# Delta mixer: filler in a bank without readers, gate mixed in the receptance loop, rate evacuated in one run, VectorE's products between value tiles

## The chip, the cores and the metric

The kernel runs on one core of one Trainium2 chip. The metric is the device time of one execution in microseconds (us). Three runs of the kernel before gave a median of 2432.17 us (2429.4 to 2437.03).

## The reference, cut to what matters

The program computes two blocks of a small network on 256 tokens of width 1024. The first block (feed-forward layers and two kinds of attention) and most of the second are not touched. The change lies in the one layer of the second block that mixes tokens with the generalised delta rule:

```
xx = x_prev - x                       # x_prev: x shifted by one token
r = (x + xx*mu[0]) @ w_rkv[0]         # receptance
k = (x + xx*mu[2]) @ w_rkv[1]         # key
v = (x + xx*mu[3]) @ w_rkv[2]         # value
xw, xa, xg = x + xx*mu[1], x + xx*mu[4], x + xx*mu[5]
w_log = -softplus(-(w0 + tanh(xw @ w1) @ w2)) - 0.5;  decay = exp(-exp(w_log))
a = sigmoid(a0 + (xa @ a1) @ a2)      # rate
g = sigmoid(xg @ g1) @ g2             # gate
kk = normalised per head(k * k_k);  k = k * (1 + (a - 1) * k_a)
# per head and token: state = state*w + (state @ -kk) outer (kk*a) + v outer k;  y = state @ r
out = group_norm(y) + (sum over the head of r*k*r_k) * v
return (out * g) @ w_o
```

The recurrence is computed in chunks of 64 tokens, from products of r, k, kk and a with exponentials of the summed decay.

## The kernel before, in words

Activations lie with the width on the partitions: a tensor of 1024 x 256 is eight tiles of 128 x 256 (`KD` = 8). A weight chunk is 128 x 1024 and holds what one output tile needs. SyncE loads chunks into a ring of eight (line 463, `weight_ring`). For float32 accuracy each chunk of the three large projections is cut into an upper part, which ScalarE writes (line 2119, `weight_upper`, four slots), and a rest, which VectorE writes (line 1395, `weight_lower`). An output tile is 24 matmuls of 128x256: lower x upper, upper x lower, upper x upper for eight tiles of input. All matmuls are issued from the helper at line 517, whatever calls it; transposes stand at line 1196.

There is no planner that runs on the chip: every engine works through an order written out by hand. One thing is placed by a rule, though. Before a wait, ScalarE and VectorE call `due`, which first cuts weight chunks up to three cuts past the chunk that TensorE had taken at the event waited for. So the place of an instruction `dve.wait_ge(*due(event))` in VectorE's text also sets where VectorE cuts the next chunks: it cuts them there and not earlier.

TensorE writes to eight PSUM banks. The helper `refill(b)` makes it wait until the readers of bank b's last content are done; `next_bank` goes round banks 0 to 3. `hold(b, n)` issues n matmuls of the identity into bank b, which nobody reads; they only keep the engine at work. Each starts with `refill(b)`.

The mixer's stages, in TensorE's order: `lora_in(3)` (decay, eight input tiles `xs_t[3]`, two fillers ahead of each), `lora_in(4)` (rate), `lora_up(3)`, the eight key tiles (project_all of items(1), the first three of them interleaved), `lora_up(4)`, `lora_in(5)` (gate), the head sums of kk, `lora_up(5)`, the eight receptance tiles with the spread of the kk norms after the fifth, the eight value tiles with the head sums of the bonus after the seventh, then `delta_core`, which begins with transposes of v (line 1196) and the spread of the bonus.

Ahead of the mixer the helper `spread_two` spreads two norms into banks 6 and 7; VectorE reads bank 7 at line 1769 when it writes the normed input `xn` (name `xn_t` in the trace), tile by tile, and the bank's reader is the event after the last tile.

VectorE's order: the mixed inputs of decay and rate (line 1889, `shifted(3, k)`, `shifted(4, k)`); for key and receptance `shifted` at line 1893 and the rest of the split at line 1428 (`shifted_halves`); then the eight tiles of the gate's input (line 1889, `shifted(5, k)`), which read what ScalarE's `part(5, k)` (line 2430) wrote; then `shifted_halves(2)` for the value; the norms of kk (lines 1919 to 1932); the scans of the decay (line 1925); and, once ScalarE has written `exp_plus` (line 2479), eight products `rkr` (line 1939), `bt` (line 1942), `ar[:, 1]` (line 1943), the copy of 32 columns `w_end` (line 1944), and after the head sums of the bonus two steps (lines 1947 and 1880) and `ar[:, 0]` (line 1950).

ScalarE, for the key: per tile two evacuations (lines 2457, 2458), the receptance's upper part `xs_upper(0, f)` (line 2134), `part(5, f)` (line 2430). Then per tile the evacuation of the rate (line 2322, `lora_raw (4, k)`) and `xs_upper(2, k)`. For the value tiles: the exponentials at lines 2478, 2479 and 2482 and the evacuations (line 2322). GpSimd does `kk` (line 2626), `before_sum` (line 2630), `k_mixed` (line 2634), `kk_a` (line 2639) and, after `bt`, `k_scaled` (line 2642) as one instruction of 128x2048.

Of the kernel before, what the change touches and what calls it, by code (L numbers as in the profile page):

```python
# [7 lines left out]
ALU = mybir.AluOpType  # L8
ACT = mybir.ActivationFunctionType
# [31 lines left out]
CH = 64  # L41
# [155 lines left out]
def program(nc, dram, out, seen, stream):  # L197

    ctx = ExitStack()
    with ctx:  # L200
# [272 lines left out]
        def _(pe):  # L473
# [660 lines left out]
            def delta_mixer(i):  # L1134
# [3 lines left out]
                def lora_in(j, wd):  # L1138
                    w, used = arrived("lora1", j - 3, KD * wd)
                    b = next_bank()  # L1140
                    for k in range(KD):
                        if j == 3:
                            hold(7, 2)
                        pe.wait_ge(*of("xs", (j, k)))
                        mn = mm(bank[0:wd, b, 0:S], w[:, k * wd:(k + 1) * wd], xs_t[j][:, k, :],
                                k == 0, k == KD - 1)
# [40 lines left out]
            def delta_core():  # L1187
# [3 lines left out]
                for m, src in enumerate((v_t, ar[:, 0], bt, kt_)):  # L1191
# [8 lines left out]
                    if m == 0:  # L1200
                        head_spread("bonus", at=4)
                        pe.wait_ge(*of("ar", 0))
                        pe.wait_ge(*of("k_scaled", 0))

# [175 lines left out]
        def _(dve):  # L1380
# [514 lines left out]

            def shifted_halves(j):

                for k in range(KD):
                    shifted(j, k)
                    for done in [k - 1] * (k > 0) + [k] * (k == KD - 1):  # L1900
                        lower(xs_hl[j], done, xs_t[j][:, done, :], ("xs_upper", (j, done)), ("xs_lower", (j, done)))

            def delta_mixer(i):
# [7 lines left out]
                dve.wait_ge(*due("rkv_raw", (4, KD - 1)))  # L1911
                shifted_halves(0)
                for k in range(KD):
                    shifted(5, k)
                dve.wait_ge(*due("rkv_raw", (1, KD - 1)))
# [20 lines left out]
                for k in range(KD):  # L1936
                    dve.wait_ge(*due("rkv", (0, k)))
                    dve.wait_ge(*due("k_mixed", k))
                    V.scalar_tensor_tensor(rkr_t[:, k, :], r_t[:, k, :], vec("r_k", k), k_t[:, k, :],
                                           ALU.mult, ALU.mult).then_inc(*did("rkr", k))  # L1940
                dve.wait_ge(*due("kk_a", 3))
                step(V.tensor_tensor(bt, aa_t, kt_, ALU.mult), [("b_scaled", 0)])
                step(V.tensor_tensor(ar[:, 1], r_t, exp_plus, ALU.mult))
                step(V.tensor_copy(w_end[:, :, :],
                                   exp_plus.rearrange("p k (c t) -> p k c t", t=CH)[:, :, :, CH - 1]))
                dve.wait_ge(*due("head_sums", "bonus"))
                step(V.tensor_copy(stat[:, 1, :], bank[:, 6, 0:QT * RH]), [("head_sums_read", "bonus")])
                widen("bonus", 1)
                dve.wait_ge(*due("exp_before", 0))
                V.scalar_tensor_tensor(ar[:, 0], kk_t, -1.0, sg_t, ALU.mult, ALU.mult).then_inc(*did("ar", 0))  # L1950
                for b in range(4):
# [152 lines left out]
        def _(act):  # L2104
# [319 lines left out]
            def delta_mixer(i):  # L2424
# [29 lines left out]
                for f in range(KD):  # L2454
# [3 lines left out]
                    A.activation(k_t[:, f, :], ps, ACT.Copy).then_inc(*did("rkv", (1, f)))  # L2458
                    xs_upper(0, f)
                    act.wait_ge(*due("xs_lower", (1, f)))  # L2460
                    part(5, f)
                for k in range(KD):
                    evac("lora_raw", (4, k), aa_t[:, k, :], "lora_out", ACT.Sigmoid, bias=vec("a0", k))
                    xs_upper(2, k)
                lora(5, P, ACT.Sigmoid)
# [9 lines left out]
                for f in range(KD):  # L2475
# [4 lines left out]
                    elif f == 2:  # L2480
                        act.wait_ge(*due("before_sum", KD - 1))
                        A.activation(sg_t, sg_t, ACT.Exp, scale=-E_HALF).then_inc(*did("exp_before", 0))
                    evac("rkv_raw", (2, f), v_t[:, f, :], "rkv")
# [80 lines left out]
        def _(pool):  # L2564
# [53 lines left out]
            for i in range(DEPTH):  # L2618
                if i == 1:
# [21 lines left out]
                    pool.wait_ge(*of("b_scaled", 0))  # L2641
                    G.tensor_tensor(kt_, kt_, k_t, ALU.mult).then_inc(*did("k_scaled", 0))
                    for n in range(4):
# [125 lines left out]
```

## Time and profile before

| | us |
|---|---|
| median of three runs | 2432.17 |
| the profiled execution | 2437.4 |
| its span | 2435.5 |
| TensorE busy in the span | 2310.4 (95%) |
| VectorE, ScalarE, GpSimd busy | 1584.6, 1173.9, 362.4 |

The chain of work that ended last is TensorE for 80% of the span, VectorE for 9%, ScalarE for 5%. The mean granted TensorE clock is 0.97 of full speed. The mixer lies between 1790 and 2100 us of the span; the change touches 1793 to 1940. In the rows below, a start is in us from the span's start, a row with xN merges N instructions that follow one another, and the bracket at the end is the idle time of that engine before it and what ended it.

### The profile page before, as it was taken

The numbers are of one execution on the slowest core, as the hardware profiler recorded it, in microseconds if no ns is written. First come the engines' busy times: TensorE is split into PE (matmuls) and PEld (weight loads), VectorE is DVE, ScalarE is ACT, GpSimd is POOL, SyncE is SP. The second block draws the span as 40 slices with busy tenths as digits, with TensorE's granted clock in tenths as the row PEclk, the third lists the DMA queues.
The fourth block names the chain that finished last, engine by engine and source line by source line (L and its number), as shares of the span: only waits on it lengthen the run. The fifth ranks groups of instructions, "written<-read, shape, count | busy, mean of one in ns | idle before, by whom it ended". The sixth has DMA issues, their size and how long they took to land.

```text
span 2435.5 us, 41847 instructions
## 1 busy us (share of the span) xinstructions
PE 2310.4 (95%) x17252; PEld 2041.5 (84%) x17252; DVE 1584.6 (65%) x2226; ACT 1173.9 (48%) x2043; POOL 362.4 (15%) x353
## 2 busy tenths in 40 slices
PE   7999998899999999988999999999989798999998
PEld 7888977788888889777888999688868788978887
DVE  5886766578778866665776686277556553545763
ACT  3654443455546544444655575365446321445542
POOL 0110012111101100210111102020222230022001
PEclk9999998899999999989999999999998899999999
DMA  7776742257758767423566544355524300333553
GB/s 268 286 261 234 257 169 96 82 187 262 241 200 289 253 225 266 169 82 102 173 224 216 174 160 161 107 170 184 180 86 131 104 3 3 123 129 119 193 181 104
DMA packets 114237, 417.19 MB, mean 171 GB/s; under 512 B 12672, under 2 KB 12928, under 8 KB 113664
## 3 DMA queue, kind: packets, MB, share of 16 engines
q1 hardware_dynamic: 113184, 409.56, 49.4%
q10 hardware_dynamic: 864, 4.96, 0.6%
q8 instruction: 138, 2.26, 0.4%
q14 instruction: 51, 0.42, 0.1%
HBM read 413.42 MB, written 1.05 MB: 170 GB/s over the span
## 4 chain that ended last, share of the span: by engine, by line
PE 80%; DVE 9%; ACT 5%; issue 4%; POOL 2%; DMA 1%; POOLq 0%; DVEq 0%; ACTq 0%
PE banks L517 79%; DVE weight_lower L1395 2%; ACT weight_upper L2119 1%; ACT heap L2238 1%; DVE weight_ring L1406 1%; POOL heap L2584 1%; PE banks L908 0%; DVE nmax L1552 0%; DVE heap L1550 0%; DVE heap L1533 0%; ACT L2153 0%; DMA consts<-consts_dram 0%; DVE xn_t L1623 0%; DMA weight_ring<-ffn_up_dram 0%; DVE silu L1617 0%
## 5 line engine op out<-in xcount | busy, mean ns | idle before, releaser
L517 PE MATMUL banks<-xn_halves,weight_upper 128*128 128x512 f32 (+1 forms) x3680 | 1016.3, 347 | 8.5 <-DVE weight_lower L1395 6.5
L1395 DVE TENSOR_TENSOR weight_lower<-weight_ring,weight_upper 128x1024 fp32r<-128x1024 f32 x580 | 736.3, 1276 | 330.0 <-ACT weight_upper L2119 328.7
L517 PE MATMUL banks<-xn_halves,weight_lower 128*128 128x256 f32 x2832 | 807.4, 285 | 23.6 <-DVE branch_a_lower L1587 13.0
L2119 ACT ACTIVATE weight_upper<-weight_ring 128x1024 fp32r<-128x1024 f32 x580 | 609.5, 1056 | 344.3 <-PE banks L517 226.1
L517 PEld LDWEIGHTS banks<-xn_halves,weight_upper 128*128 128x128 f32 x3680 | 648.5, 193 | 97.5 <-DVE weight_lower L1395 6.8
L517 PEld LDWEIGHTS banks<-xn_halves,weight_lower 128*128 128x128 f32 x2832 | 544.5, 192 | 32.6 <-DVE branch_a_lower L1587 15.1
L517 PE MATMUL banks<-hidden,weight_upper 128*128 128x512 f32 x1216 | 429.2, 398 | 4.9 <-DVE heap L1474 4.2
L517 PE MATMUL banks<-hidden,weight_lower 128*128 128x256 f32 x1216 | 341.4, 281 | 0.0
L517 PEld LDWEIGHTS banks<-hidden,weight_upper 128*128 128x128 f32 x1216 | 228.3, 188 | 61.8 <-DVE heap L1474 5.2
L2584 POOL TENSOR_TENSOR heap<-heap 128x256 f32<-128x256 f32 x120 | 121.4, 1016 | 960.8 <-ACT heap L2335 634.0
L517 PEld LDWEIGHTS banks<-hidden,weight_lower 128*128 128x128 f32 x1216 | 229.7, 189 | 0.0
L1406 DVE CUSTOM_DVE_ANT_0 weight_ring<-weight_ring,c_rows,vecs 128x1024 f32<-128x1024 f32 x144 | 187.3, 1302 | 32.5 <-DMA weight_ring<-w_ada_dram 30.1
L517 PE MATMUL banks<-heap 64*64 64x64 f32 (+10 forms) x2432 | 184.4, 265 | 16.9 <-ACT heap L2244 4.8
L517 PEld LDWEIGHTS banks<-heap 64*64 64x64 f32 (+5 forms) x2432 | 154.0, 151 | 44.1 <-issue 29.1
L2573 POOL TENSOR_TENSOR heap<-heap 128x256 f32<-128x256 f32 x88 | 68.0, 772 | 511.3 <-ACT heap L2182 510.7
L517 PE MATMUL banks<-heap,weight_ring 64*64 64x15 f32 (+3 forms) x944 | 119.6, 295 | 0.0
L517 PE MATMUL banks<-consts 128*128 128x128 f32 x816 | 110.4, 290 | 5.4 <-DVE xn_t L1769 5.4
L517 PEld LDWEIGHTS banks<-heap,weight_ring 64*64 64x64 f32 (+3 forms) x944 | 96.3, 162 | 22.1 <-issue 5.9
L517 PEld LDWEIGHTS banks<-consts 128*128 128x128 f32 x816 | 102.7, 203 | 9.4 <-issue 8.9
L2177 ACT ACTIVATE heap<-banks 128x512 f32<-128x512 f32 x88 | 52.5, 597 | 116.6 <-PE banks L517 116.6
L1474 DVE TENSOR_TENSOR heap<-banks,heap 128x512 f32<-128x512 f32 x88 | 60.8, 691 | 47.6 <-ACT heap L2177 47.6
L2238 ACT ACTIVATE heap<-heap,nmax 128x256 f32<-128x256 f32 (+2 forms) x128 | 52.0, 408 | 60.9 <-DVE nmax L1555 60.8
(287 smaller groups left out, 2605.7 us busy)
## 6 DMA issues: line engine op xcount, KB each, us to landing
weight_ring<-w_ada_dram SPq DMA_DIRECT2D x144, 512.0 KB, 4.4
weight_ring<-ffn_gate_dram SPq DMA_DIRECT2D x88, 512.0 KB, 3.6
weight_ring<-ffn_up_dram SPq DMA_DIRECT2D x88, 512.0 KB, 3.6
weight_ring<-ffn_down_dram SPq DMA_DIRECT2D x88, 512.0 KB, 3.5
weight_ring<-m_w_up_dram SPq DMA_DIRECT2D x64, 512.0 KB, 3.7
weight_ring<-m_w_down_dram SPq DMA_DIRECT2D x64, 512.0 KB, 3.7
weight_ring<-w_in_dram SPq DMA_DIRECT2D x58, 512.0 KB, 4.3
weight_ring<-b_w_rkv_dram SPq DMA_DIRECT2D x24, 512.0 KB, 3.6
```

The source lines that it names most:

```text
L517: return nc.tensor.matmul(o, w, r, start=first, stop=last)
L1395: V.tensor_tensor(w_lo[:, n % RING, :], ring[:, n % RING, :], w_hi[:, j % SPLITS, :].bitcast(F32), ALU.subtract).then_inc(*did("weight_low ...
L1406: V.tensor_tensor_reduce(w, w, c_rows[:, :], half, vec("b_ada", i), ALU.mult, ALU.add, mod[:, i:i + 1]).then_inc(*did("ada_mod", i, also=[ ...
L1474: V.tensor_tensor(gu[:, f % 4], bank[:, b:b + 2, 0:S], gu[:, f % 4], ALU.add).then_inc(*did("gate_up", (s, f)))
L2119: A.activation(w_hi[:, j % SPLITS, :], ring[:, n % RING, :], ACT.Copy).then_inc(*did("weight_upper", j))
L2177: A.activation(gu[:, f % 4], bank[:, b:b + 2, S:2 * S], ACT.Copy).then_inc(*did("gate_up_half", (s, f)))
L2238: A.activation(s_, s_, ACT.Exp, bias=nmax[:, u % 2, j:j + 1], accum_out=den[:, u % 2, j:j + 1]).then_inc(*did("exp", (l, u, j), also=[("ex ...
L2573: G.tensor_tensor(gu[:, f % 4, 0, :], gu[:, f % 4, 0, :], gu[:, f % 4, 1, :], ALU.mult).then_inc(*did("hidden", (s, f)))
L2584: G.tensor_tensor(acc, acc, sum_tile(n, what, f), ALU.add).then_inc(*did("sum_added", (n, what, f)))
```

## The change

- Filler: the two fillers ahead of each input tile of `lora_in(3)` go to bank 5, not bank 7.
- Gate: `shifted(5, k)` moves from a loop of its own into the loop of `shifted_halves(0)`, right behind `shifted(0, k)`. On ScalarE `part(5, f)` now stands ahead of `xs_upper(0, f)`.
- Rate: ScalarE evacuates the eight tiles `lora_raw (4, k)` in one run, and writes the eight `xs_upper(2, k)` behind them.
- Products: VectorE gets waits on the evacuated value tile 0 ahead of `bt`, tile 2 ahead of `ar[:, 1]`, tile 3 ahead of `ar[:, 0]`, which moves ahead of the bonus steps. The copy `w_end` moves to ScalarE, behind the exponential of line 2482. GpSimd's `k_scaled` becomes eight instructions of 128x256; TensorE waits for the last.

```diff
 lora_in, TensorE
-                            hold(7, 2)
+                            hold(5, 2)
 delta_core, TensorE
-                        pe.wait_ge(*of("k_scaled", 0))
+                        pe.wait_ge(*of("k_scaled", KD - 1))
 VectorE
-            def shifted_halves(j):
+            def shifted_halves(j, other=None):
                 for k in range(KD):
                     shifted(j, k)
+                    if other:
+                        shifted(other, k)
                     for done in [k - 1] * (k > 0) + [k] * (k == KD - 1):
                         lower(xs_hl[j], done, ...)
...
-                shifted_halves(0)
-                for k in range(KD):
-                    shifted(5, k)
+                shifted_halves(0, 5)
...
+                dve.wait_ge(*due("rkv", (2, 0)))
                 dve.wait_ge(*due("kk_a", 3))
                 step(V.tensor_tensor(bt, aa_t, kt_, ALU.mult), [("b_scaled", 0)])
+                dve.wait_ge(*due("rkv", (2, 2)))
                 step(V.tensor_tensor(ar[:, 1], r_t, exp_plus, ALU.mult))
-                step(V.tensor_copy(w_end[:, :, :], exp_plus...[:, :, :, CH - 1]))
+                dve.wait_ge(*due("rkv", (2, 3)))
+                dve.wait_ge(*due("exp_before", 0))
+                V.scalar_tensor_tensor(ar[:, 0], kk_t, -1.0, sg_t, ALU.mult, ALU.mult).then_inc(*did("ar", 0))
                 dve.wait_ge(*due("head_sums", "bonus"))
                 step(V.tensor_copy(stat[:, 1, :], bank[:, 6, 0:QT * RH]), [("head_sums_read", "bonus")])
                 widen("bonus", 1)
-                dve.wait_ge(*due("exp_before", 0))
-                V.scalar_tensor_tensor(ar[:, 0], kk_t, -1.0, sg_t, ALU.mult, ALU.mult).then_inc(*did("ar", 0))
 ScalarE
-                    xs_upper(0, f)
                     act.wait_ge(*due("xs_lower", (1, f)))
                     part(5, f)
+                    xs_upper(0, f)
                 for k in range(KD):
                     evac("lora_raw", (4, k), aa_t[:, k, :], "lora_out", ACT.Sigmoid, bias=vec("a0", k))
+                for k in range(KD):
                     xs_upper(2, k)
...
-                        A.activation(sg_t, sg_t, ACT.Exp, scale=-E_HALF).then_inc(*did("exp_before", 0))
+                        A.activation(sg_t, sg_t, ACT.Exp, scale=-E_HALF)
+                        act.wait_ge(*due("exp_plus", 0))
+                        A.activation(w_end[:, :, :], exp_plus...[:, :, :, CH - 1],
+                                     ACT.Copy).then_inc(*did("exp_before", 0))
 GpSimd
-                    G.tensor_tensor(kt_, kt_, k_t, ALU.mult).then_inc(*did("k_scaled", 0))
+                    for k in range(KD):
+                        G.tensor_tensor(kt_[:, k, :], kt_[:, k, :], k_t[:, k, :], ALU.mult).then_inc(
+                            *did("k_scaled", k))
```

## Rows read from the trace of the kernel before

**Rows 1.** The waits view, TensorE alone, 1785 to 1965 us: total, times, longest.
```profile
PE banks L517 <- DVE weight_lower L1395: 11.5, 1, 11.5
PE banks L517 <- DVE xn_t L1769: 5.4, 1, 5.4
```
**Rows 2.** The timeline, TensorE, lora_in(3) and lora_in(4).
```profile
1798.39 1.19 PE L517 MATMUL banks<-consts 128*128 128x128 f32 x4 [5.37 <-DVE xn_t L1769]
...
1802.68 0.71 PE L517 MATMUL banks<-consts 128*128 128x128 f32 x4
...
1809.40 4.10 PE L517 MATMUL banks<-heap,weight_ring 128*64 128x256 f32 x18
```
**Rows 3.** The timeline, VectorE: inputs (line 1889) of xs_t[3], then of xs_t[4].
```profile
1793.40 0.48 DVE L1889 SCALAR_TENSOR_TENSOR heap<-xn_t,vecs,heap 128x255 f32<-128x255 f32 x1
...
1794.58 0.85 DVE L1889 SCALAR_TENSOR_TENSOR heap<-xn_t,vecs,heap 128x255 f32<-128x255 f32 x1
...
1797.78 0.47 DVE L1769 SCALAR_TENSOR_TENSOR xn_t<-x_t,vecs,banks 128x256 f32<-128x256 f32 x1
...
1800.56 4.03 DVE L1889 SCALAR_TENSOR_TENSOR heap<-xn_t,vecs,heap 128x255 f32<-128x255 f32 x8
```
**Rows 4.** Stretches of 2 us: engines' busy (xcount), granted clock, DMA share, GB/s.
```profile
1796.00:1798.00 2.00, 0.00 (x0) 0.00 (x0) 2.00 (x6) 1.37 (x3) 2.00 (x4) 0.50 0.00 0
1846.00:1848.00 2.00, 1.33 (x5) 0.59 (x4) 2.00 (x3) 1.46 (x5) 1.01 (x1) 1.00 0.65 238
1908.00:1910.00 2.00, 0.00 (x0) 0.00 (x0) 2.00 (x2) 2.00 (x4) 0.00 (x0) 1.00 0.71 258
```
**Rows 5.** The timeline, TensorE: the end of lora_up(4), lora_in(5), lora_up(5).
```profile
1852.18 2.92 PE L517 MATMUL banks<-silu,weight_ring 64*128 64x256 f32 x6 [3.98 <-ACT heap L2322]
1855.04 6.43 PE L517 MATMUL banks<-heap,weight_ring 128*128 128x256 f32 x16
...
1865.55 6.28 PE L517 MATMUL banks<-silu,weight_ring 128*128 128x256 f32 x16
```
**Rows 6.** The timeline, VectorE: part of a round of the key loop, then the gate's inputs.
```profile
1842.37 0.83 DVE L1428 TENSOR_TENSOR shifted_lower<-heap,shifted_upper 128x256 fp32r<-128x256 f32 x1
...
1843.52 1.21 DVE L1395 TENSOR_TENSOR weight_lower<-weight_ring,weight_upper 128x1024 fp32r<-128x1024 f32 x1
...
1847.69 3.23 DVE L1889 SCALAR_TENSOR_TENSOR heap<-xn_t,vecs,heap 128x255 f32<-128x255 f32 x8
```
**Rows 7.** The timeline, ScalarE: the last key round's start, then the rate's tiles.
```profile
1844.65 1.11 ACT L2119 ACTIVATE weight_upper<-weight_ring 128x1024 fp32r<-128x1024 f32 x1
...
1846.92 0.53 ACT L2322 ACTIVATE heap<-banks,vecs 128x256 f32<-128x256 f32 x1
1851.35 0.42 ACT L2134 ACTIVATE shifted_upper<-heap 128x256 fp32r<-128x256 f32 x1 [3.89 <-DVE heap L1893]
1851.68 0.46 ACT L2322 ACTIVATE heap<-banks,vecs 128x256 f32<-128x256 f32 x1
```
**Rows 8.** The timeline, ScalarE, VectorE and GpSimd around TensorE's pause in the value tiles.
```profile
1904.28 1.04 ACT L2119 ACTIVATE weight_upper<-weight_ring 128x1024 fp32r<-128x1024 f32 x1
...
1904.41 3.90 DVE L1939 SCALAR_TENSOR_TENSOR xn_t<-heap,vecs 128x256 f32<-128x256 f32 x8 [5.28 <-ACT heap L2479]
...
1910.60 6.60 POOL L2642 TENSOR_TENSOR heap<-heap 128x2048 f32<-128x2048 f32 x1 [5.34 <-DVE heap L1942]
...
1912.88 4.36 DVE L1944 COPY w_end<-heap 128x32 f32<-128x32 f32 x1
1917.27 4.63 DVE L1395 TENSOR_TENSOR weight_lower<-weight_ring,weight_upper 128x1024 fp32r<-128x1024 f32 x4
```
**Rows 9.** The timeline, TensorE: the bonus sums and the first transposes.
```profile
1931.68 3.63 PE L517 MATMUL banks<-consts,xn_t 128*128 128x2 f32 x32
...
1940.56 1.94 PE L1196 MATMUL banks<-consts,heap 128*128 128x128 f32 x16 [0.78 <-ACT heap L2322]
```
**Rows 10.** The timeline, VectorE: a cut in the receptance loop, beside GpSimd's work.
```profile
1876.60 1.68 DVE L1395 TENSOR_TENSOR weight_lower<-weight_ring,weight_upper 128x1024 fp32r<-128x1024 f32 x1 [2.14 <-ACT weight_upper L2119]
```

More of the change, by code:

```diff
@@ L1940, in delta_mixer @@
                                            ALU.mult, ALU.mult).then_inc(*did("rkr", k))
+                dve.wait_ge(*due("rkv", (2, 0)))
                 dve.wait_ge(*due("kk_a", 3))
                 step(V.tensor_tensor(bt, aa_t, kt_, ALU.mult), [("b_scaled", 0)])
+                dve.wait_ge(*due("rkv", (2, 2)))
                 step(V.tensor_tensor(ar[:, 1], r_t, exp_plus, ALU.mult))
-                step(V.tensor_copy(w_end[:, :, :],
-                                   exp_plus.rearrange("p k (c t) -> p k c t", t=CH)[:, :, :, CH - 1]))
+                dve.wait_ge(*due("rkv", (2, 3)))
+                dve.wait_ge(*due("exp_before", 0))
+                V.scalar_tensor_tensor(ar[:, 0], kk_t, -1.0, sg_t, ALU.mult, ALU.mult).then_inc(*did("ar", 0))
                 dve.wait_ge(*due("head_sums", "bonus"))
@@ L2481, in delta_mixer @@
                         act.wait_ge(*due("before_sum", KD - 1))
-                        A.activation(sg_t, sg_t, ACT.Exp, scale=-E_HALF).then_inc(*did("exp_before", 0))
+                        A.activation(sg_t, sg_t, ACT.Exp, scale=-E_HALF)
+                        act.wait_ge(*due("exp_plus", 0))
+                        A.activation(w_end[:, :, :], exp_plus.rearrange("p k (c t) -> p k c t", t=CH)[:, :, :, CH - 1],
+                                     ACT.Copy).then_inc(*did("exp_before", 0))
                     evac("rkv_raw", (2, f), v_t[:, f, :], "rkv")
```

## The prediction

> **What bounds the kernel now.** The page comes first: TensorE is busy 95% of the span and carries 80% of the chain that ended last, so a change to the mixer pays only where TensorE stands still or works at a low clock. The waits view of TensorE names two pauses, 11.5 us for a cut weight chunk and 5.4 us for line 1769 [rows 1]; the timeline adds a third, 3.98 us for an evacuation of ScalarE [rows 5], and places all three.
>
> Pause A lies ahead of `lora_in(3)`: TensorE idles from 1793.0 to 1798.39 [rows 2]. Its releaser is the last normed tile, written by 1798.25, although the first input xs_t[3] is there at 1793.88 [rows 3]. TensorE doesn't wait for data; it waits to overwrite bank 7 with filler. Pause B lies in `lora_up(4)` and ends at 1852.18 [rows 5]. Followed back: the bank wants the rate's second evacuation (1851.68), which stands behind an `xs_upper(2, 0)` that waited 3.89 us for VectorE [rows 7], which ran the eight gate tiles from 1847.69 to 1850.9 first [rows 6]. Pause C, 11.5 us from 1907.1 on, lies behind the third value tile: VectorE doesn't come to cutting the fourth value chunk before 1917.27, and TensorE starts when the first of four cuts is done, at 1918.55 [rows 1, 8].
>
> Pauses also cost clock. Late in A the granted clock is at the lower level (1.2 GHz) [rows 4]; a round of fillers and one input tile then takes 2.15 us (two from 1798.39 to 1802.68), and 1.21 at the upper level (2.4 GHz), as in the five and a half up to 1809.40 [rows 2]. Behind B a matmul of 128x256 takes 0.40 (16 in 6.43) where 0.23 (18 in 4.10) is the upper level's [rows 2, 5].
>
> **The change, part by part.** Times are on the axis of the execution before; a gain in one stage moves the later ones as a block.
>
> *Filler in bank 5.* Bank 5 held nothing but filler just before, so the wait goes, and what is late next is the input. TensorE starts at 1793.0; tile 0 is there at 1793.88 and tile 1 at 1795.43, so rounds 0 and 1 end near 1794.6 and 1796.1. From there on inputs come every 0.8 us, the last near 1800.1 [rows 3], faster than a round of 1.21: six rounds end at 1803.4. `lora_in(4)` is 16 matmuls of 0.225, 3.6 us, and ends at 1807.0; its inputs are all there by 1804.6 [rows 3]. Before, it ended at 1813.5 [rows 2]. **Gain 6.5**, and not more, since work and inputs fill the stretch. The other end: should the clock fall in the thin first rounds for as long as it was low before, two rounds cost 0.9 more each: 4.6.
>
> *Gate in the receptance loop, rate in one run.* The eight gate tiles cost VectorE 3.2 us wherever they stand; what counts is what waits behind them. In the key loop VectorE's lines 1428 and 1893 take 1.15 from start to start (1842.37 to 1843.52) and the cut 1.13, a round of 2.28 [rows 6]; ScalarE's round is 2.27 (1844.65 to 1846.92) [rows 7]. Both catch up behind TensorE's 2.88 (24 matmuls of 0.12), since the first three key tiles come at once. With a gate tile (0.40) VectorE's round is 2.68, still under 2.88, so key tiles aren't starved. But `xs_upper(0, f)` waits for VectorE, so ScalarE falls to its pace in the last five rounds: at most 2.0 us later, and I take 1.4, because `part(5, f)` now fills some of that wait. The first rate evacuation comes at 1848.3, not 1846.92 [rows 7]. Nothing stands between the eight any more, at 0.36 each, so `lora_up(4)` gets its last bank near 1849.9 and `lora_in(5)` starts at 1850.5, not 1855.04: 4.5 saved. What the clock adds is open. If it stays up, `lora_in(5)` takes 3.6 and not 6.4, but another thing ends last then: the value's upper parts now follow the evacuations, VectorE makes their inputs from about 1850.9 in eight rounds of 0.73, to 1856.8, and the gate's Sigmoid stands behind them on ScalarE, at 1857. So `lora_up(5)` starts no earlier than 1857.0 to 1857.8, where it was 1865.55 [rows 5], and the head sums ahead of it may pull the clock down, as the bonus sums do: the value tile behind them takes 4.6, not 2.9 (1935.2 to 1939.8) [rows 9]. That caps the gain at 8.6. Ends 4.5 (clock as before) and 8.6; I take the middle, since TensorE would be half busy and never long idle from 1846 to 1850.5, and a stretch like that kept its clock (1846 to 1848 [rows 4]). **Gain 6.5.** The moved uppers cost nothing for the value tiles, which come 40 us later; without that cover they would cost what they take, eight of 0.35.
>
> *Products between value tiles.* Before, VectorE is done with `rkr` at 1908.3; `bt` takes 2.29, up to GpSimd's release at 1910.60, `ar[:, 1]` as long, and the copy of 32 columns 4.36 [rows 8]. The copy ends at 1917.24 and GpSimd's `k_scaled` at 1917.20: the copy stood waiting for GpSimd. Now the wait on value tile 0 (evacuated right behind the upper cut of 1904.28, so no wait in fact) makes VectorE cut the fourth chunk at 1908.3, and the tile starts at 1909.6: a pause of 2.5 us for 11.5. Then come `bt` (to 1911.8), two cuts, `ar[:, 1]`, a cut, `ar[:, 0]`, a cut, with eight instructions of GpSimd beside them. A cut takes 1.21 alone [rows 6] and 1.68 beside GpSimd [rows 10]; I charge each VectorE instruction behind `bt` with a whole piece of GpSimd, 0.7 (an eighth of some 5 us, what is left of 6.60 when `ar[:, 1]`'s share is off it). The cuts end at 1913.8, 1915.7 and, behind `ar[:, 1]` (1918.7), at 1920.6. Value tiles 3 to 6 run 1909.6 to 1912.5, 1913.8 to 1916.7, to 1919.6, and 1920.6 to 1923.5. The bonus sums take 3.5 and the last tile 4.6 [rows 9]: 1931.6, for 1939.8. **Gain 8.2.** Without the charge for GpSimd the count gives 1929.9, a gain of 9.9; with the clock down after the short pause (the four tiles from 1918.55 took 13.1 to 1931.68, not 11.5) it gives 6.6. `w_end` costs ScalarE less than an evacuation of 256 columns, 0.36, and is hidden by TensorE's next tile; uncovered it would cost that. `ar[:, 0]` ends earlier than before, and the last piece of `k_scaled` is wanted only behind the first transposes.
>
> The Trainium skill, SBUF — State Buffer, section SBUF: two separate sides, says that VectorE and GpSimd share one port pair as an exclusive lock, for a VectorE instruction with two SBUF inputs too, and the loser stands still for the other's whole instruction. It speaks against `k_scaled` in eight: each piece is one more turn that a cut can lose. By it the value stage gives between the 8.2 and the 9.9 just worked out. The trace agrees: the copy ends with GpSimd's instruction.
>
> Sum: 6.5 + 6.5 + 8.2 = 21.2 us; ends 4.6 + 4.5 + 6.6 = 15.7 and 6.5 + 8.6 + 9.9 = 25.0. The profiled execution took 2437.4 (1.9 around its span); its like would take 2416.2. It stands 5.2 above the median of 2432.2, which becomes 2411.0.
>
> **The rivals.**
> - *The key loop tips over.* If both the cut (1.68) and line 1428 wait for GpSimd, VectorE's round is 1.68 + 1.15 + 0.40 = 3.2. Five rounds of 3.2, not 2.28, put the first rate evacuation at 1851.5: pause B is moved, not removed, and that stage gives 0.7. In all 15.4: 2416.8. For it: neither engine has slack there [rows 6, 7]. Against: the present round holds one such wait already.
> - *Clock not kept.* Fed in pieces, TensorE stays at the lower level: eight rounds of 2.15 and 7.2 for `lora_in(4)` end at 1817.4, 4.0 later than now; the others give their low ends. 7.1 in all: 2425. Against: the same pattern ran at the upper level from 1802.7 on [rows 2], and 1 to 3 us into pause C the clock was still up [rows 4].
> - *The filler's wait stays*, because bank 5 has a reader after all: 14.7 in all, 2417.5. The text of the kernel speaks against it.
> - *Slower.* The lower clock spreads over every stage that is fed in pieces: 4.0 lost at `lora_in`; key tiles 4 to 8 at 0.213 a matmul, 5.1 a tile, 11.2 lost; the value stage gives nothing (1909.6 + 4 x 5.1 + 4.4 + 5.1 = 1939.5); 4.5 of the rate stage is left. 10.7 slower: 2443. It decides where VectorE's key round passes 2.88 and each tile starts with a pause. Against: TensorE would still be busy 90% there.
>
> **How the numbers follow.** Forecast 0.72; key loop 0.12; clock not kept 0.06; filler 0.03; slower 0.04; more than 25 us, by a clock that is up throughout, 0.03. The predicted time is the forecast's, 2411. Its ends are 2407.2 and 2416.5; key loop and filler lie at 2416.8 and 2417.5; with 3 us for the scatter of medians the range is 2404 to 2420, which leaves out the clock rivals. About 0.3% (7.3 us) can be told from no change: faster 0.72 + 0.12 + 0.03 + 0.03 = 0.90, within it 0.06, slower 0.04.
>
> **What would show it.** Right: no wait for line 1769 in TensorE's waits view; waits for `weight_lower` in the value tiles of 2 to 5 us in all, the longest near 2.5; ScalarE's eight rate evacuations 0.36 apart; `k_scaled` as eight pieces with cuts of 1.7 or more beside them. Wrong: a granted clock of 0.5 from `lora_in(5)` through `lora_up(5)` (then that stage gives 4.5), a late cut in the key loop, or the time won handed back at a wait in `delta_core`, which I don't see.

## The result, and the profile after

The changed kernel is faster, by less than forecast. Over six runs each, measured side by side, its median is 2419.1 us (2410.7 to 2425.5) and that of the kernel before 2434.2: a ratio of 0.9935, interval 0.991 to 0.996, or 15 us. Forecast were 2411 and 21 us. The profiled execution took 2425.5 us with a span of 2423.5; forecast for its like were 2416.2.

TensorE's waits over the same stretch (who waited for whom: total, times, longest):

```profile
PE banks L517 <- DVE weight_lower L1395: 2.7, 2, 2.4
PE banks L517 <- ACT heap L2459: 1.2, 1, 1.2
PE banks L517 <- ACT heap L2323: 1.2, 2, 0.9
PE banks L517 <- DVE heap L1889: 0.7, 2, 0.5
```

Against [rows 1], the wait for line 1769 is gone, that for cut chunks fell from 11.5 to 2.7, and pause B (3.98 in [rows 5]) became two of 1.2 and 0.9. The lines of ScalarE and GpSimd moved by one to six: 2119 is now 2120, 2322 is 2323, 2642 is 2648.

TensorE's timeline of the changed kernel, from the last fillers to `lora_up(3)`, and then the rate and gate stage:

```profile
1792.50 3.29 PE L517 MATMUL banks<-consts 128*128 128x128 f32 x28
1796.25 0.65 PE L517 MATMUL banks<-heap,weight_ring 128*64 128x256 f32 x2 [0.46 <-DVE heap L1889]
...
1809.13 1.99 PE L517 MATMUL banks<-silu,weight_ring 64*128 64x256 f32 x8
...
1840.98 1.56 PE L517 MATMUL banks<-silu,weight_ring 64*128 64x256 f32 x6
1843.78 0.91 PE L517 MATMUL banks<-silu,weight_ring 64*128 64x256 f32 x2 [1.24 <-ACT heap L2459]
1845.60 3.78 PE L517 MATMUL banks<-silu,weight_ring 64*128 64x256 f32 x8 [0.91 <-ACT heap L2323]
1849.31 6.20 PE L517 MATMUL banks<-heap,weight_ring 128*128 128x256 f32 x16
1855.35 4.60 PE L517 MATMUL banks<-consts,heap 128*128 128x2 f32 x32
1859.81 6.07 PE L517 MATMUL banks<-silu,weight_ring 128*128 128x256 f32 x16
```

Stage A is clean: the fillers run straight on, and the wait for the first input is 0.46 us. The rate stage is not: `lora_in(5)` and `lora_up(5)` take about as long as in [rows 5].

The value tiles: the timeline of ScalarE, VectorE, GpSimd and TensorE, to set beside [rows 8, 9].

```profile
1902.25 1.21 DVE L1395 TENSOR_TENSOR weight_lower<-weight_ring,weight_upper 128x1024 fp32r<-128x1024 f32 x1
1902.53 0.26 ACT L2486 ACTIVATE w_end<-heap 128x32 f32<-128x32 f32 x1
1903.38 2.27 DVE L1943 TENSOR_TENSOR heap<-heap 128x2048 f32<-128x2048 f32 x1
1905.69 2.90 DVE L1395 TENSOR_TENSOR weight_lower<-weight_ring,weight_upper 128x1024 fp32r<-128x1024 f32 x2
1905.74 13.64 POOL L2648 TENSOR_TENSOR heap<-heap 128x256 f32<-128x256 f32 x8 [6.47 <-DVE heap L1943]
1908.52 2.82 DVE L1945 TENSOR_TENSOR heap<-heap 128x2048 f32<-128x2048 f32 x1
...
1903.51 0.38 PE L517 MATMUL banks<-shifted_upper,weight_lower 128*128 128x256 f32 x1 [2.41 <-DVE weight_lower L1395]
1906.97 0.38 PE L517 MATMUL banks<-shifted_upper,weight_lower 128*128 128x256 f32 x1 [0.33 <-DVE weight_lower L1395]
1916.05 3.94 PE L517 MATMUL banks<-consts,xn_t 128*128 128x2 f32 x32
1926.10 1.94 PE L1196 MATMUL banks<-consts,heap 128*128 128x128 f32 x16 [0.78 <-ACT heap L2323]
```

VectorE cuts right behind `rkr`, the long pause is 2.41 us, and the copy costs ScalarE 0.26.

To compare kernels I cut the stretch at starts of TensorE's instructions in each timeline; "whole" runs from the first normed tile (line 1769) to the first transposes. Microseconds:

| kernel | first normed tile to lora_up(3) | to first key tile | to lora_up(4) | to lora_in(5) | to receptance | to bonus sums | to transposes | whole |
|---|---|---|---|---|---|---|---|---|
| before | 22.4 | 6.7 | 24.5 | 10.5 | 16.5 | 60.2 | 8.9 | 149.5 |
| after | 15.8 | 6.7 | 25.1 | 8.3 | 16.2 | 50.5 | 10.1 | 132.7 |
| filler_only | 15.8 | 6.7 | 25.0 | 10.5 | 13.4 | 60.3 | 8.9 | 140.4 |
| gate_rate_only | 23.0 | 6.7 | 24.8 | 8.3 | 16.0 | 60.0 | 8.9 | 147.8 |
| products_only | 23.0 | 6.7 | 24.8 | 10.4 | 13.3 | 50.5 | 8.9 | 137.6 |
| after_again | 15.8 | 6.7 | 25.9 | 8.3 | 13.4 | 50.5 | 8.9 | 129.5 |
| rate_fillers | 15.8 | 6.7 | 25.2 | 6.7 | 12.1 | 51.1 | 7.4 | 124.9 |
| one_k_scaled | 15.8 | 6.7 | 25.7 | 8.3 | 13.2 | 54.3 | 10.1 | 134.2 |
| copy_on_vector | 15.8 | 6.7 | 25.7 | 8.3 | 13.3 | 51.2 | 10.4 | 131.3 |
| no_waits | 15.8 | 6.7 | 24.6 | 7.1 | 16.5 | 56.4 | 8.9 | 136.0 |
| gate_apart | 15.8 | 6.7 | 25.2 | 6.4 | 12.2 | 51.1 | 7.4 | 124.7 |
| late_sums | 15.8 | 6.7 | 25.7 | 8.3 | 13.3 | 55.0 | 4.4 | 129.2 |
| key_fillers | 15.8 | 7.2 | 23.2 | 6.7 | 13.7 | 50.5 | 10.1 | 127.2 |
| gate_apart_fillers | 15.8 | 7.2 | 23.2 | 5.8 | 12.1 | 51.1 | 7.4 | 122.5 |

In late_sums the bonus sums stand behind the eighth value tile, so its last two columns count differently. Within a column the entries of kernels with the same edit there mostly agree to 0.1 us. The columns that don't (to lora_up(4), to receptance, to transposes) are those where the clock changes, and they differ between two traces of one and the same kernel (after, after_again) by up to 3 us. Single entries of the others move with the clock too. In no_waits, the 7.1 ahead of `lora_in(5)` stands beside 8.3 in six traces with the same code there: the pauses are as long, but the clock fell only 1.3 us behind the second of them, and the last eight matmuls of `lora_up(4)` took 2.56 us and not 3.78. The first column has 22.4 and 23.0 without the filler's edit.

### The profile page after: what moved, and what is told of

Same layout as the page of the kernel before. It is cut to its first block, busy times and chain, and to the rows that moved or that the text cites. A ratio compares the mean times of both kernels' runs of the same rounds, so it can differ in the third digit from the quotient of the medians.

```text
span 2423.5 us, 41857 instructions
## 1 busy us (share of the span) xinstructions
PE 2314.7 (96%) x17252; PEld 2042.7 (84%) x17252; DVE 1581.6 (65%) x2225; ACT 1173.8 (48%) x2044; POOL 369.3 (15%) x360
## 4 chain that ended last, share of the span: by engine, by line
PE 81%; DVE 8%; ACT 4%; issue 4%; POOL 2%; DMA 1%; POOLq 0%; DVEq 0%; ACTq 0%
PE banks L517 80%; DVE weight_lower L1395 2%; ACT heap L2239 1%; DVE weight_ring L1406 1%; POOL heap L2589 1%; ACT weight_upper L2120 1%; PE banks L908 0%; DVE nmax L1552 0%; DVE heap L1550 0%; DVE heap L1533 0%; ACT L2154 0%; DMA weight_ring<-ffn_up_dram 0%; DMA c_rows<-c_rows_dram 0%; PE banks L1196 0%; ACT heap L2284 0%
## 5 line engine op out<-in xcount | busy, mean ns | idle before, releaser
L517 PEld LDWEIGHTS banks<-xn_halves,weight_lower 128*128 128x128 f32 x2832 | 545.5, 193 | 32.3 <-DVE branch_a_lower L1587 15.1
```

The lines of the kernel that those rows point to most:

```text
L517: return nc.tensor.matmul(o, w, r, start=first, stop=last)
```

## The experiments

**Each part alone, and the changed kernel once more on the same chip.** The edits are the hunks of the diff.

`filler_only`:

```diff
-                            hold(7, 2)
+                            hold(5, 2)
```

> The kernel before with one edit: the fillers of lora_in(3) go to bank 5. From the first normed tile to the start of lora_up(3) the kernel before takes 22.4 us. My theory (TensorE waited to overwrite bank 7, not for data): 15.8, and the 6.6 us stay won up to the transposes (149.5 becomes 142.9, or up to 2 us off that by the clock); the run is 0.2 to 0.3% faster, 5 to 7 us. Rival (bank 7 was not what it waited for): 22.4 and no change.

Measured: 2430.7 us, ratio 0.9977 (0.9961 to 0.9993), and 15.8 us in the first column. The wait for line 1769 is gone from its waits view. The 6.6 us are there, in this kernel and in every one with the edit (15.8 in the table). The whole is 9.1 us shorter, more than the 2 us of margin that I gave: 3.1 of it lie between `lora_in(5)` and the receptance, where nothing was edited.

`gate_rate_only` has the gate tiles in the loop of `shifted_halves(0, 5)`, ScalarE's changed order, and the rate in one run.

```diff
-                shifted_halves(0)
-                for k in range(KD):
-                    shifted(5, k)
+                shifted_halves(0, 5)
```

> The kernel before with the edits on the gate and the rate alone. From the start of lora_up(4) to the start of lora_in(5) it takes 10.5 us before and 8.3 in the changed kernel; from there to the first receptance tile 16.5 and 16.2. My theory (the pause is shorter, but the clock falls all the same): 8.3 and 16.2 again, 2 us in all. Rival (this edit is worth 4.5 to 8.6 by itself, as forecast, and was spoiled by the phase that the filler's edit gave it): 4 to 8 us less over the two stretches.

Measured: 2437.7 us, ratio 1.000 (0.9976 to 1.0023); 8.3 and 16.0 in its two columns. The theory holds: this part is worth 2.1 us, by itself as in company, too little for the medians. The phase of the other edits didn't spoil it.

`products_only` has the waits, the order, the copy on ScalarE and the eight pieces.

```diff
+                dve.wait_ge(*due("rkv", (2, 0)))
...
+                dve.wait_ge(*due("rkv", (2, 2)))
...
-                    G.tensor_tensor(kt_, kt_, k_t, ALU.mult).then_inc(*did("k_scaled", 0))
+                    for k in range(KD):
+                        G.tensor_tensor(kt_[:, k, :], kt_[:, k, :], k_t[:, k, :], ALU.mult).then_inc(
+                            *did("k_scaled", k))
```

> The kernel before with the edits of the value tiles alone (waits, order, the copy on ScalarE, GpSimd in eight pieces). From the first receptance tile to the transposes the kernel before takes 69.1 us, the changed one 60.6. Theory: 60.6 here too, 8.5 us by itself, since the stage doesn't lean on the other edits; the run 0.3 to 0.35% faster. Rival (part of it came from the earlier stages): under 6 us.

Measured: 2427.6 us, ratio 0.9957 (0.9936 to 0.9978). From the receptance to the transposes 59.4 us, 9.7 less than before: the part doesn't lean on the others. In every kernel that keeps this part whole and the sums in their place, the bonus sums come 9.1 or 9.7 earlier; the rest is the clock of the last value tile (8.9, 10.1 or 7.4 in the last column).

`after_again` is the changed kernel, without an edit.

> The changed kernel, unchanged, on the same chip as the three parts. If the parts add up: 6.6 + 2 + 8.5 = 17 us from the first normed tile to the transposes, 149.5 becoming 132.7, and 15 us in the medians. If the parts overlap or spoil one another by the clock, the sum of the three alone differs from this by over 2 us.

Measured: 2421.8 us, ratio 0.9933 (0.991 to 0.9955), and 129.5 for the whole, 20.0 less than before, not 16.8. The three parts alone give 9.1 + 1.8 + 11.9 = 22.8, over 2 us off. Both gaps are one column: from `lora_in(5)` to the receptance. Without it the parts give 6.1 + 1.3 + 8.8 = 16.2 and the whole edit 16.5 and 16.9. So the parts add up, and the clock deals out 3 us on top. TensorE's timeline of after_again:

```profile
1851.44 3.78 PE L517 MATMUL banks<-silu,weight_ring 64*128 64x256 f32 x8 [1.12 <-ACT heap L2323]
1855.15 5.02 PE L517 MATMUL banks<-heap,weight_ring 128*128 128x256 f32 x16
1860.00 3.63 PE L517 MATMUL banks<-consts,heap 128*128 128x2 f32 x32
1863.49 5.39 PE L517 MATMUL banks<-silu,weight_ring 128*128 128x256 f32 x16
```

The last three took 6.20, 4.60 and 6.07 above, the same instructions behind nearly the same pauses (1.25 and 1.12 us here, 1.24 and 0.91 there).

**Keeping TensorE at work in lora_up(4).**

```diff
 lora_up
                     for f in range(KD):
+                        if j == 4 and f in (3, 4):
+                            hold(5, 5)
                         b = next_bank()
```

> The changed kernel with five fillers into bank 5 ahead of the fourth and of the fifth matmul of lora_up(4), where TensorE pauses 1.24 and 0.91 us. Theory (the clock, lost in these pauses, is the term that was mis-sized): the granted clock stays 1.0 through lora_in(5), which takes 3.6 us and not 6.0; the stretch from the start of lora_up(4) to the first receptance tile goes from 24.5 to 18 to 21, 4 to 6 us won. Rival (ScalarE's pace sets it: evacuations, then uppers of the value ahead of the gate's Sigmoid): lora_in(5) gets faster but lora_up(5) starts as late as before, under 1.5 us won.

Measured: 2413.4 us, ratio 0.9894 (0.984 to 0.9949), an interval that reaches the changed kernel's 0.9935; the time won is read from the traces. In TensorE's timeline of rate_fillers five fillers show as ten instructions:

```profile
1842.99 1.38 PE L517 MATMUL banks<-consts 128*128 128x128 f32 x10
1844.32 0.70 PE L517 MATMUL banks<-silu,weight_ring 64*128 64x256 f32 x2
1844.94 1.38 PE L517 MATMUL banks<-consts 128*128 128x128 f32 x10
1846.26 1.99 PE L517 MATMUL banks<-silu,weight_ring 64*128 64x256 f32 x8
1848.18 3.72 PE L517 MATMUL banks<-heap,weight_ring 128*128 128x256 f32 x16
```

Two stretches of 2 us of the same kernel, and then two of the changed one: the stretch and its length, busy times of TensorE, weight loads, VectorE, ScalarE and GpSimd, the granted clock, DMA share, GB/s. A clock of 1.00 is the upper level, 2.4 GHz, and 0.50 the lower, 1.2.

```profile
1846.00:1848.00 2.00, 2.00 (x11) 1.55 (x10) 2.00 (x6) 2.00 (x7) 0.00 (x0) 1.00 0.00 0
1848.00:1850.00 2.00, 2.00 (x10) 1.63 (x9) 1.17 (x4) 1.42 (x5) 0.00 (x0) 1.00 0.35 63
```
```profile
1846.00:1848.00 2.00, 2.00 (x6) 1.52 (x6) 1.73 (x5) 1.41 (x4) 0.00 (x0) 0.50 0.00 0
1850.00:1852.00 2.00, 2.00 (x6) 1.58 (x5) 1.77 (x5) 1.10 (x4) 0.00 (x0) 0.50 0.74 248
```

The same eight matmuls take 1.99 and not 3.78, and the sixteen of `lora_in(5)` 3.72 and not 6.20. From the start of `lora_up(4)` to the receptance it is 18.8 us, against 24.5 and 21.7 in the two traces of the changed kernel. The fillers add matmuls and win 2.9 to 5.7 us: the clock was the larger part of what the stage lost, and the rival (ScalarE's pace, under 1.5 us) falls. The clock then falls behind the head sums, so `lora_up(5)` still takes 5.2.

**The value stage taken apart.** Three kernels from the changed one.

```diff
-                        pe.wait_ge(*of("k_scaled", KD - 1))
+                        pe.wait_ge(*of("k_scaled", 0))
...
-                    for k in range(KD):
-                        G.tensor_tensor(kt_[:, k, :], kt_[:, k, :], k_t[:, k, :], ALU.mult).then_inc(
-                            *did("k_scaled", k))
+                    G.tensor_tensor(kt_, kt_, k_t, ALU.mult).then_inc(*did("k_scaled", 0))
```

> The changed kernel with k_scaled as one instruction of 128x2048 again. If GpSimd's instruction and VectorE's of two SBUF inputs exclude each other for whole instructions: k_scaled starts at bt's end and runs some 4.4 us, the cuts of value tiles 4 and 5 stand behind it, and TensorE gets a second pause of about 2.5 to 3 us ahead of value tile 4; the stretch from the receptance's start to the transposes is 2 to 3 us longer than the 60.6 of the changed kernel. If they share: no more than 0.5 us longer, and the cuts are only slower by a part.

Measured: 2426.8 us, ratio 0.9956 (0.9927 to 0.9986); from the receptance to the transposes 64.4, not 60.6: 3.8 longer. The timeline of VectorE, GpSimd and TensorE:

```profile
1899.83 6.75 DVE L1395 TENSOR_TENSOR weight_lower<-weight_ring,weight_upper 128x1024 fp32r<-128x1024 f32 x2
1899.87 5.62 POOL L2647 TENSOR_TENSOR heap<-heap 128x2048 f32<-128x2048 f32 x1 [6.47 <-DVE heap L1943]
...
1906.63 0.43 PE L517 MATMUL banks<-shifted_upper,weight_lower 128*128 128x256 f32 x1 [2.39 <-DVE weight_lower L1395]
```

Two cuts that take 2.4 alone took 6.75, so 4.4 went into standing behind GpSimd; its 5.62 are 1.2 of waiting for the first cut and those 4.4 of work. One stood still while the other worked. The pause of 2.39 us is the one expected; the stretch was to be 2 to 3 us longer and is 3.8, and what goes beyond the pause is clock, at 0.50 from 1908 to 1910. The Trainium skill, SBUF — State Buffer, section SBUF: two separate sides, states such an exclusive lock for the whole instruction; this trace agrees (6.75 = 2 x 1.2 + 4.4).

```diff
+                step(V.tensor_copy(w_end[:, :, :],
+                                   exp_plus.rearrange("p k (c t) -> p k c t", t=CH)[:, :, :, CH - 1]))
...
-                        A.activation(sg_t, sg_t, ACT.Exp, scale=-E_HALF)
-                        act.wait_ge(*due("exp_plus", 0))
-                        A.activation(w_end[:, :, :], exp_plus.rearrange("p k (c t) -> p k c t", t=CH)[:, :, :, CH - 1],
-                                     ACT.Copy).then_inc(*did("exp_before", 0))
+                        A.activation(sg_t, sg_t, ACT.Exp, scale=-E_HALF).then_inc(*did("exp_before", 0))
```

> The changed kernel with the copy of 32 columns back on VectorE, behind ar[:, 1]; waits and eight pieces kept. Theory (the 4.36 us were a wait for GpSimd's one long instruction): the copy now takes at most one piece of GpSimd, under 1.3 us, and the stretch from the receptance's start to the transposes stays within 1 us of 60.6. Rival (such a copy is slow by itself): 4 us and a pause of TensorE of 2 us or more.

Measured: 2417.0 us, ratio 0.9925 (0.9895 to 0.9956); 61.6 us in the stretch, 1.0 longer. VectorE's timeline:

```profile
1899.72 0.60 DVE L1946 COPY w_end<-heap 128x32 f32<-128x32 f32 x1
```

The same copy of 32 columns took 4.36 in [rows 8]. It was never slow; it waited for GpSimd. Once GpSimd works in pieces, moving the copy to ScalarE is worth 0.7 us up to the bonus sums (50.5 for 51.2); the last column differs by the clock.

`no_waits`:

```diff
-                dve.wait_ge(*due("rkv", (2, 0)))
                 dve.wait_ge(*due("kk_a", 3))
...
-                dve.wait_ge(*due("rkv", (2, 2)))
...
-                dve.wait_ge(*due("rkv", (2, 3)))
```

> The changed kernel without the three new waits on value tiles in VectorE's text, all else kept. If the waits do the placing of the cuts: VectorE cuts the fourth value chunk only behind bt, ar[:, 1] and ar[:, 0], near 7 to 9 us after rkr ends, and TensorE's pause is 8 to 10 us in place of 2.4; the stretch from the receptance's start to the transposes is 6 to 8 us longer than 60.6. If the moved copy was what mattered, it is at most 2 us longer.

Measured: 2424.3 us, ratio 0.9933 (0.9905 to 0.9961); 65.3 in the stretch, 4.7 longer, with one pause of 7.5 us. VectorE's timeline:

```profile
1910.41 2.29 DVE L1943 TENSOR_TENSOR heap<-heap 128x2048 f32<-128x2048 f32 x1
1912.73 3.29 DVE L1395 TENSOR_TENSOR weight_lower<-weight_ring,weight_upper 128x1024 fp32r<-128x1024 f32 x2
1915.95 2.81 DVE L1945 SCALAR_TENSOR_TENSOR heap<-spare,heap 128x2048 f32<-128x2048 f32 x1
```

The waits do the placing, but I expected a pause of 8 to 10 and a stretch 6 to 8 us longer: I had overlooked that the wait for `exp_before`, which now stands ahead of `ar[:, 0]`, carries a value tile too, and `due` cuts two chunks there. The 4.7 us stand in one trace; the medians (0.9933 here, 0.9933 and 0.9935 for the changed kernel) don't show them.

**Gate and rate taken apart.** `gate_apart` is the changed kernel with the gate's loop and ScalarE's order as before:

```diff
-                shifted_halves(0, 5)
+                shifted_halves(0)
+                for k in range(KD):
+                    shifted(5, k)
...
+                    xs_upper(0, f)
                     act.wait_ge(*due("xs_lower", (1, f)))
                     part(5, f)
-                    xs_upper(0, f)
```

> The changed kernel with the eight gate tiles back in a loop of their own on VectorE and the order of ScalarE's two steps in the key loop as before; the rate stays in one run. If the run of evacuations alone removes pause B: from the start of lora_up(4) to the start of lora_in(5) it takes 8.3 us or less (6.5 to 8.3), since ScalarE comes out of the key loop 1.5 us earlier without the extra round of VectorE. If the gate's mixing in the loop was needed, TensorE waits for the gate's inputs or banks there: over 9 us.

Measured: 2418.2 us, ratio 0.989 (0.9858 to 0.9923), and 6.4 us from `lora_up(4)` to `lora_in(5)`, not 8.3. TensorE's timeline there:

```profile
1832.25 0.70 PE L517 MATMUL banks<-silu,weight_ring 64*128 64x256 f32 x2 [0.31 <-ACT heap L2459]
1833.32 3.52 PE L517 MATMUL banks<-silu,weight_ring 64*128 64x256 f32 x8 [0.37 <-ACT heap L2323]
```

Two stretches of 2 us of the same kernel, columns as above:

```profile
1832.00:1834.00 2.00, 1.38 (x4) 0.89 (x5) 2.00 (x4) 2.00 (x7) 1.01 (x1) 0.90 0.54 203
1834.00:1836.00 2.00, 2.00 (x6) 1.55 (x5) 2.00 (x6) 1.27 (x3) 0.00 (x0) 0.50 0.00 0
```

The pauses are 0.31 and 0.37, and not 1.24 and 0.91 as in the changed kernel. So the run of evacuations alone removes pause B, and mixing the gate into the key loop costs 1.9 us there (with fillers in the pauses 0.9: 6.7 in rate_fillers, 5.8 in the last kernel below). The clock fell here all the same, behind pauses that sum to 0.7 us. It doesn't always: the kernel before has the same two pauses, 0.30 and 0.37 us, ahead of 1846.45 and 1847.51, and its clock was still 1.00 from 1848 to 1850.

**The bonus sums behind the last value tile.**

```diff
-                    if f == KD - 2:
+                    if f == KD - 1:
                         head_sums("bonus", rkr_t, "rkr")
```

> The changed kernel with the head sums of the bonus behind the eighth value tile, not the seventh. In the kernels so far the matmuls of two columns are followed by a value tile at the lower clock (4.6 to 5.1 us in place of 2.9). If the sums pull the clock down: the last value tile takes 2.9, from the end of the seventh value tile to the first transposes it takes 7 us and not 8.9 to 10, 2 to 3 us won, of which the transposes, then at the lower clock, may give back up to 2. If the clock has another cause there: no change beyond 0.5 us.

Measured: 2422.3 us, ratio 0.9918 (0.9892 to 0.9944). TensorE's timeline:

```profile
1916.54 0.39 PE L517 MATMUL banks<-shifted_upper,weight_lower 128*128 128x256 f32 x1 [1.29 <-DVE weight_lower L1395]
1919.52 4.57 PE L517 MATMUL banks<-consts,xn_t 128*128 128x2 f32 x32
1923.95 3.65 PE L1196 MATMUL banks<-consts,heap 128*128 128x128 f32 x16
...
1931.65 1.91 PE L1196 MATMUL banks<-consts,heap 128*128 128x128 f32 x16
```

The last value tile takes 2.98 us (1916.54 to 1919.52), the upper clock's pace, and the clock falls inside the sums. But the tile now waits 1.29 for its cut, and the transposes take the low stretch: 3.65 for the 1.94 above. From the receptance to the second run of transposes it is 67.1 us here and 65.9 in the changed kernel. The low stretch moves with the sums; nothing is won.

The sums don't bring it every time, though. In rate_fillers, gate_apart and gate_apart_fillers the same sums (3.63 us) are followed by a value tile of 3.1 us, the upper clock's pace: the 7.4 in the last column. In these three the clock had fallen earlier, 1.2 to 1.3 us into the value tile behind the pause of 2.4 us, for 3.4 us; in the other kernels with that pause it stayed up in this tile. Two stretches of 2 us of gate_apart, columns as above:

```profile
1889.00:1891.00 2.00, 2.00 (x11) 2.00 (x11) 1.97 (x3) 0.00 (x0) 1.80 (x2) 0.50 0.00 0
1904.00:1906.00 2.00, 2.00 (x19) 2.00 (x18) 1.19 (x1) 0.00 (x0) 0.00 (x0) 1.00 0.00 0
```

So late_sums shows that the low stretch behind the sums goes where they go, and not that they bring one each time. Where the clock falls, behind the short pause or behind the sums, is decided by something that the traces don't show.

**Fillers ahead of the key tiles**, on top of those in `lora_up(4)`:

```diff
+                        if j == 3 and f > 3:
+                            hold(5, 1)
...
                 lora_up(3, RN)
+                hold(5, 5)
                 project_all(items(1), xs_hl[1], ("xs_lower", 1))
```

> The kernel with fillers in lora_up(4), and in addition one filler ahead of each of the last four matmuls of lora_up(3) and five ahead of the first key tile, where TensorE idles 1.2 to 1.7 us. From the first key matmul to the start of lora_up(4) it took 24.5 to 25.9 us in nine traces, 23.0 would be eight tiles of 2.88. If the clock falls in the thin stretch ahead of the key tiles: 23.1 to 23.4, 1.5 to 2.5 us won. If the fillers only delay the first key matmul: it starts 0.5 us or more later after lora_up(3)'s start (6.7 so far) and the tiles take as long as before.

Measured: 2415.2 us, ratio 0.9886 (0.9862 to 0.991). The key tiles take 23.2 us in place of 25.2, and start 0.55 later: 1.5 won in the trace. Both halves of the expectation came true. The interval can't tell it from rate_fillers.

**Together.** The changed kernel with the gate apart, three fillers for five in `lora_up(4)`, and those of key_fillers.

```diff
                         if j == 4 and f in (3, 4):
-                            hold(5, 5)
+                            hold(5, 3)
```

> The changed kernel with the gate's loop apart again, three fillers ahead of the fourth and the fifth matmul of lora_up(4), one ahead of each of the last four of lora_up(3), and five ahead of the first key tile. If the late start of the rate's evacuations and the clock are the two things that the rate stage lost: from the start of lora_up(4) to the start of lora_in(5) 5.2 to 5.9 us (6.4 with the gate apart alone, 6.7 with fillers alone, 8.3 changed), lora_in(5) 3.6, and the whole from the first normed tile to the transposes 123 to 126 us in place of 129.5 to 132.7; the run 1.1 to 1.3% faster than before. Rival (the clock falls there whatever is done, since the pauses were short in the kernel with the gate apart and it fell all the same): lora_in(5) 4.7 to 6.3, and no better than 0.7 to 1.0%.

Measured: 2405.6 us over six runs (2397.3 to 2412.9), ratio 0.9859 (0.9836 to 0.9881). It is the fastest kernel here, 33 us ahead of the kernel before and about twice as far ahead of it as the changed kernel. TensorE's timeline:

```profile
1838.86 0.70 PE L517 MATMUL banks<-silu,weight_ring 64*128 64x256 f32 x2
1839.49 0.94 PE L517 MATMUL banks<-consts 128*128 128x128 f32 x6
1840.35 1.99 PE L517 MATMUL banks<-silu,weight_ring 64*128 64x256 f32 x8
1842.27 3.72 PE L517 MATMUL banks<-heap,weight_ring 128*128 128x256 f32 x16
```

`lora_in(5)` is at the upper level again, so the rival is out. The 5.8 us ahead of it lie in the expected range; the whole (122.5) and the ratio (1.4% faster) came out a little better than expected. The whole is 10.2 us shorter than in the profiled changed kernel and 7.0 shorter than in after_again.

## Why the prediction was right, and where it was off

The range held the median (2419.1, top end 2420), the sign and the order of size were right, and the point was 8 us low. That the range held, by 0.9 us, is in part luck: gate and rate gave 1.7 us, far below the low end of 4.5 that the range was added up from, and the other two parts, a little above their forecasts, made up for it in part. The kernel before measured 2434.2 and not 2432.2, so the gain itself was 6 us short, 15 for 21. Step by step, in the two profiled executions:

- *Filler in bank 5*: forecast 6.5, measured 22.4 - 15.8 = 6.6, the same in every kernel with the edit. The cause, that TensorE waited to overwrite bank 7, is shown by filler_only.
- *Gate and rate*: forecast 6.5 with ends 4.5 and 8.6; measured 1.7 up to the receptance: 2.1 at `lora_up(4)`, 0.2 behind it, less 0.7 in the key tiles, whose low stretch was longer. This is the step that failed. ScalarE's delay was right: the first rate evacuation lies 4.1 us behind the start of `lora_up(4)` (1845.09 and 1840.98), for a forecast 3.7. What failed is the sentence that they then come 0.36 apart and `lora_in(5)` starts at 1850.5. ScalarE's timeline of the changed kernel:

```profile
1845.09 1.55 ACT L2323 ACTIVATE heap<-banks,vecs 128x256 f32<-128x256 f32 x4
1846.86 0.47 ACT L2323 ACTIVATE heap<-banks,vecs 128x256 f32<-128x256 f32 x1 [0.21 <-PE banks L517]
1847.71 0.47 ACT L2323 ACTIVATE heap<-banks,vecs 128x256 f32<-128x256 f32 x1 [0.38 <-PE banks L517]
```

  From the fifth on they come 0.85 apart and wait for TensorE, which had dropped to the lower level in the two pauses, before `lora_in(5)` and not behind it. The sign that I had named against myself, a granted clock of 0.5 from `lora_in(5)` on, came too, but with a gain of 1.7 and not 4.5. My low end had priced the low clock from `lora_in(5)` on, but not in `lora_up(4)`; rate_fillers shows 1.99 for the 3.78 there. And I took the pauses as harmless since a thin stretch had kept its clock in [rows 4]. gate_apart shows a clock that fell behind pauses of 0.7 us in all.
- I also booked the gate's mixing as the price of a gain. It is a price only: gate_apart does without it and is 1.9 us better at that place in the trace (the intervals of the medians overlap). I had worked out its delay (1.4) and never asked what the loop bought.
- *Products*: forecast 8.2, measured 69.1 - 60.6 = 8.5. The first pause was right (2.5 and 2.41). Behind it two errors cancelled, which is luck. The charge of 0.7 for GpSimd per VectorE instruction was too high: the two cuts took 2.90 (2.44 alone), `ar[:, 1]` 2.82 (2.29), so the second pause was 0.33, not 1.3, and the third didn't come. That brought the bonus sums 1.5 us earlier than forecast. Against that the sums and the last tile took 9.3, not 8.1, by the clock (10.1 and 8.9 with the 0.78 us of waiting ahead of the transposes).
- The stretch gave 16.8 of the forecast 21.2. In the profiled executions another 4.8 went elsewhere: 2.3 before the stretch began (1793.37 for 1791.05), in code that is the same, and 2.5 behind it, 1.8 of these by 2046 us, where from 2000 to 2050 the granted clock was 0.93 and 1.00 before. The profiled execution is also the slowest of the changed kernel's six. after_again gave 20.0 in the stretch. The medians' 15 and 15.1 us are consistent with 16.8 in the stretch within their interval (9.7 to 21.9 us).
- The rivals: the key loop didn't tip over (no wait for a cut chunk in the key tiles, and a first rate evacuation 0.4 us later than forecast, not 3.2); the clock rival had the right cause, in the wrong stage and at a smaller price; the filler's wait went; nothing points to a slower kernel.

What stays open: what decides whether the stage from `lora_in(5)` takes 13.3 or 16.2 us in one execution, and whether the clock falls in the value tile behind the pause or behind the bonus sums. The traces show both for identical code or identical TensorE work and don't show the cause.

## What to carry to other kernels

Ask of each filler which bank it writes, and who still reads that bank. In a kernel whose queues cut weights inside their waits, the place of a wait is a schedule: put one ahead of each long instruction that would otherwise stand before the next cut. And where TensorE is fed in pieces, count its matmuls at the lower clock as the low end, from the first pause on: here a few fillers in pauses of 0.9 and 1.2 us won 2.9 to 5.7 us in the trace, and shortening pause B by two edits had won 2.1.

## What the runs showed of the hardware

- The granted clock falls in stretches in which TensorE is busy throughout in the profile: the 32 matmuls of two columns of the bonus sums (3.6 us at the upper level) are followed by the lower level in 11 of the 14 traces, late_sums among them, where the low stretch moved with them. In the other three they are not, and there the clock had fallen some 12 us before the sums.
- How long the lower level lasts once TensorE is at full work again differs: in the kernel before 2.9 us at the start of the key tiles (1820.1 to 1823.0), and 8.4 in the stage of [rows 5] (1852.2 to 1860.6).
- Identical instructions (from `lora_in(5)` to the receptance) took 13.2 to 13.4 us in six traces without fillers there, 16.0 to 16.5 in four, and 12.2 in gate_apart; with fillers 12.1, 12.1 and 13.7. The Trainium skill, TensorE: Matmul & The Clock Gate, section What's actually happening, says that the chip's watch on activity runs free of the kernel, so that the same kernel changes level at other places from run to run. The two traces of the changed kernel agree with it (16.2 and 13.4 us), though neither shows that this is the cause.
- A VectorE instruction with two SBUF inputs and one of GpSimd exclude each other: in one_k_scaled one long GpSimd instruction held two cuts for 4.4 us. The copy of 32 columns, which reads one input only, stood still too (4.36 us in [rows 8], 0.60 beside short pieces). With eight short pieces VectorE lost 0.2 to 0.5 us an instruction, and GpSimd took 13.6 us for what takes 4.4 as one instruction.
